# Where a decoder layer turns the 128 tiles of its expert table: eight moved into the first expert pass, fewer in earlier stages, and one input loaded ahead of a barrier

## The chip, the cores and the metric

The kernel runs on one core of one Trainium2 chip. The metric is the device time of one execution in microseconds (us). TensorE multiplies, VectorE, ScalarE and GpSimd (POOL) work on tiles in on-chip memory, and DMA transfers are issued from the queues of SyncE (SP), ScalarE and POOL.

## The reference

One layer of a decoder for 512 prompt tokens and 32 sample tokens (544 columns), then a final norm.

```python
h = rmsnorm(x, norm_mix)
proj = h @ w_in                        # feeds three branches and their gates
h_ml = mlstm_chunkwise(...)            # (A) matrix memory, 4 heads
y_rw, ... = rwkv7_branch(...)          # (B) 8 heads, ends with a norm by groups
y_xa = memory_attention(q, mk, mv)     # (C) mk, mv = projections of rmsnorm(mem_prompt)
x = x + jnp.sum(gates * bproj, axis=2) @ w_out
x = x + peer(rmsnorm(x, norm_ffn), pk_wq, pk_k1, pk_k2, pk_u, pk_v)

def peer(...):                         # per token, 8 heads
    v1, i1 = top_k(s1, 16); v2, i2 = top_k(s2, 16)
    top, pos = top_k(cand, 16)         # 16 of the 16384 experts per head
    gate = softmax(top)
    act = gelu(einsum('thkd,td->thk', u_tab[eidx], xb))
    return einsum('thk,thkd->td', gate * act, v_tab[eidx])
```

## The kernel before, in words

Five instruction streams, one an engine, are written out by hand and meet at semaphores. The stages follow each other, four of them closed by a barrier of all engines:

1. First branch (mLSTM): projections, a convolution on VectorE in eight steps, then a loop over four heads. `exponents(0)` on VectorE opens that loop.
2. Second branch (RWKV-7): chunks on small matrices, the sample tokens, then a norm by groups for each of four pairs of heads (`ym`, `xq`, `yv`, `g` on TensorE).
3. Memory attention: it loads the memory tokens (`MEM`, 1 MB), squares them on ScalarE, norms and projects them.
4. Gates, merge and output projection.
5. Queries: for 16 half heads TensorE makes queries and scores, and VectorE selects the best 16 (`choose(i)`, of which `top16` is the work). `choose(0)` to `choose(13)` stand here; in steps 1 to 8 VectorE also makes one low part of the layer's input (`XL`).
6. First pass: 128 slots. The kernel computes 416 tokens densely: tile `s` of the expert table `u` (512 KB) is loaded by SP into a ring of three buffers (`RAW`), split into a high half by ScalarE (`HI`) and a low half by VectorE (`low_part`, `LO`), two slots ahead of its 24 products on TensorE. `low_part` frees the ring's buffer for the next load. Beside that VectorE finishes the top-k for five groups of tokens (`top_part`, eight parts each, placed by `part_slot`), and 104 units of one-hot matrices (`one_hots`, placed by `hots_slot`) go from VectorE to ScalarE to TensorE and back through ScalarE into a gate table of 13 x 2 MB.
7. Second pass: the same with table `v`, 128 slots.

For the last 128 tokens the first pass doesn't use the dense product: their experts' rows are gathered and multiplied on VectorE (`dot`, 128 of them, spread by `dotted_by`). Gathering wants rows, and the input holds `u` by columns. So every one of the 128 tiles of `u` is also turned: POOL loads it (`turn_tiles`), VectorE transposes it by blocks (`turn_tile`), and POOL writes it to the table `u_rows` in four DMAs. That is side work laid into all the stages before the first gather. `TILES` says how: per phase the first tile, how many, and how many buffers they go through (depth). `turn_tile` waits for its tile's load and for the writes of the tile `depth` before it; the load in turn waits until that tile is turned. VectorE works in order, so a `turn_tile` that waits holds all that is written behind it.

Line 1657 is the transposition, 520 and 525 are POOL's load and writes of it, 1060 every product, 2125 `low_part`, 2092 to 2102 `top16`, 2258 `one_hots`, 2267 `dot`.

## Time and profile before

| | us |
|---|---|
| median of 3 runs | 2743.36 |
| lowest, highest | 2740.65, 2758.79 |
| the profiled execution | 2741.5 |
| its span, first to last instruction | 2739.8 |
| TensorE, VectorE, ScalarE, POOL busy | 2399.8, 1724.2, 913.8, 695.7 |

All rows come from the one profiled execution. Its time is 1.7 us above its span, and a saving read from the rows is taken off its time. Busy times are shares over stages with different limits: that VectorE is busy for 63% of the span says nothing about a stage in which it is the last to finish. In the rows "idle before" is how long the engine stood before the instruction, with what ended that.

### The profile page before, as it was taken

To read this page: it belongs to the slowest core of one execution; us is meant where nothing else is said; L and a number is where in the kernel's file an instruction comes from. 1 tells how busy PE (TensorE), PEld (TensorE's weight loads), DVE (VectorE), ACT (ScalarE), POOL (GpSimd) and SP (SyncE) were. 2 spreads that over 40 slices of the span, in tenths; PEclk is the share of its full clock that TensorE was granted. 3 is DMA by queue.
4 is the path that set the end of the run, shared out by engine and by line. 5 is a ranking of instruction groups with operands and counts; after the bars stand their busy time and mean duration, and the time that the engine had idled before them with its cause. 6 is when DMAs were issued, how large, how long until landed. Compare 5 with 4: busy or idle time off the path is not lost.

```text
span 2739.8 us, 41344 instructions
## 1 busy us (share of the span) xinstructions
PE 2399.8 (88%) x16321; PEld 2205.8 (81%) x16321; DVE 1724.2 (63%) x3186; ACT 913.8 (33%) x1569; POOL 695.7 (25%) x1011
## 2 busy tenths in 40 slices
PE   7956886887567989889669978999999999999997
PEld 5944665885456988878569977999999999999997
DVE  3545266434542444445878877777876577787876
ACT  3212143220011111122124455767775333333332
POOL 3310000001330555424520100333333123232320
PEclk9967897996787999999889989999999999999999
DMA  4620320012653899748655544999999889999993
GB/s 145 188 82 16 105 54 24 19 34 82 237 180 103 278 289 301 249 143 260 219 189 190 180 143 141 307 332 332 321 323 365 294 304 338 346 350 347 341 346 125
DMA packets 324337, 590.67 MB, mean 216 GB/s; under 512 B 26832, under 2 KB 217312, under 8 KB 322608
## 3 DMA queue, kind: packets, MB, share of 16 engines
q1 hardware_dynamic: 222960, 274.07, 30.5%
q0 software_dynamic: 82752, 286.69, 30.4%
q10 hardware_dynamic: 18432, 27.27, 2.7%
q8 instruction: 130, 2.13, 0.3%
q14 instruction: 63, 0.52, 0.1%
HBM read 459.28 MB, written 128.64 MB: 215 GB/s over the span
## 4 chain that ended last, share of the span: by engine, by line
PE 50%; DVE 22%; DMA 15%; issue 5%; ACT 5%; POOL 3%; ACTq 0%; DVEq 0%; POOLq 0%
PE PS L1060 49%; DMA GU<-u_rows,EIDX 4%; DMA RAW<-in_uT 3%; DMA u_rows<-arena 3%; DMA u_rows<-CBLK 3%; DVE arena L1623 3%; POOL u_rows L525 3%; DVE OH L2258 2%; DVE LO L2125 2%; DVE GU L2267 1%; DMA u_rows<-TQ 1%; ACT HI L964 1%; ACT OH L1002 1%; DVE arena L1657 1%; ACT arena L691 1%
## 5 line engine op out<-in xcount | busy, mean ns | idle before, releaser
L2125 DVE TENSOR_TENSOR LO<-RAW,HI 128x1024 fp32r<-128x1024 f32 x256 | 313.1, 1224 | 239.6 <-ACT HI L964 239.0
L964 ACT ACTIVATE HI<-RAW 128x1024 fp32r<-128x1024 f32 x256 | 270.1, 1056 | 538.8 <-PE PS L1060 508.7
L1060 PE MATMUL PS<-XH,HI 128*128 128x416 f32 x1024 | 373.5, 365 | 39.8 <-issue 39.8
L1060 PE MATMUL PS<-HT,W 128*128 128x272 f32 (+1 forms) x1536 | 381.0, 410 | 18.5 <-DVE HT L1669 12.4
L1060 PEld LDWEIGHTS PS<-HT,W 128*128 128x128 f32 (+1 forms) x1536 | 296.4, 194 | 96.9 <-issue 18.4
L1060 PE MATMUL PS<-XH,LO 128*128 128x416 f32 x1024 | 366.2, 358 | 0.0
L1060 PE MATMUL PS<-XL,HI 128*128 128x416 f32 x1024 | 364.2, 356 | 0.0
L1060 PE MATMUL PS<-WH,HI 128*128 128x416 f32 x1024 | 361.0, 353 | 2.0 <-DVE WL L2140 2.0
L1060 PE MATMUL PS<-WL,HI 128*128 128x416 f32 x1024 | 360.3, 352 | 0.0
L1060 PE MATMUL PS<-WH,LO 128*128 128x416 f32 x1024 | 358.0, 350 | 0.0
L1060 PE MATMUL PS<-arena 64*64 64x64 f32 (+10 forms) x3864 | 276.5, 260 | 69.3 <-DVE arena L1623 23.8
L1060 PEld LDWEIGHTS PS<-arena 64*64 64x64 f32 (+3 forms) x3864 | 220.2, 153 | 112.7 <-DVE arena L1623 30.2
L660 POOL DMA_INDIRECT GU<-u_rows,EIDX x128 | 157.9, 1233 | 567.0 <-DVE ACTG L2267 488.2
L668 POOL DMA_INDIRECT GROW<-in_vT,EIDX x128 | 155.3, 1213 | 408.1 <-DVE ACC L2283 311.5
L1060 PEld LDWEIGHTS PS<-XH,HI 128*128 128x128 f32 x1024 | 197.5, 193 | 42.1 <-issue 40.2
L1060 PEld LDWEIGHTS PS<-XL,HI 128*128 128x128 f32 x1024 | 197.5, 193 | 2.8
L1060 PEld LDWEIGHTS PS<-XH,LO 128*128 128x128 f32 x1024 | 196.2, 192 | 2.1
L1060 PEld LDWEIGHTS PS<-WH,HI 128*128 128x128 f32 x1024 | 192.5, 188 | 4.2 <-issue 2.3
L1060 PEld LDWEIGHTS PS<-WH,LO 128*128 128x128 f32 x1024 | 193.1, 189 | 2.4
L1060 PEld LDWEIGHTS PS<-WL,HI 128*128 128x128 f32 x1024 | 192.7, 188 | 1.1
L2267 DVE CUSTOM_DVE_ANT_0 GU<-GU,XTOK 128x1024 f32<-128x1024 f32 x128 | 155.2, 1222 | 57.4 <-DMA GU<-u_rows,EIDX 57.0
L1002 ACT ACTIVATE OH<-OH,IT 128x128 f32<-128x128 f32 x416 | 131.7, 391 | 154.1 <-DVE OH L2258 153.2
(261 smaller groups left out, 3647.3 us busy)
## 6 DMA issues: line engine op xcount, KB each, us to landing
RAW<-in_uT SPq DMA_DIRECT2D x128, 512.0 KB, 5.0
RAW<-in_vT SPq DMA_DIRECT2D x128, 512.0 KB, 5.8
arena<-in_uT POOLq DMA_DIRECT2D x92, 512.0 KB, 5.1
W<-in_w_in SPq DMA_DIRECT2D x58, 512.0 KB, 4.9
u_rows<-arena POOLq DMA_DIRECT2D x228, 128.0 KB, 3.9
table_a<-AX ACTq DMA_DIRECT2D x128, 208.0 KB, 4.6
gate_table<-GST SPq DMA_DIRECT2D x13, 2048.0 KB, 14.3
AIN<-table_a SPq DMA_DIRECT2D x128, 208.0 KB, 6.6
```

The lines of the kernel that those rows point to most:

```text
L525: pool.dma_start(rows[q], turned[32 * q:32 * q + 32].rearrange("c (b x) -> c b x", b=4)).then_inc(S(f"tout{k % 2}"), 16)
L660: pool.indirect_dma_start(out=GU[j % NGU][0:NGT], out_offset=None, in_=flat_u, in_offset=bass.IndirectOffsetOnAxis(ap=EIDX[0:NGT, 1, j:j + ...
L668: pool.indirect_dma_start(out=GROW[0:NGT, j % NGR, :], out_offset=None, in_=flat_v, in_offset=bass.IndirectOffsetOnAxis(ap=EIDX[0:NGT, 0, ...
L691: step(nc.scalar.activation(out, in_, func, **kw), sem)
L964: nc.scalar.activation(HI[:, s % NRING], RAW[:, s % NRING], ACT.Copy).then_inc(S("hi"), 1)
L1002: ins = nc.scalar.activation(hot, hot, ACT.Copy, scale=IT[:, 2, 4 * u + x:4 * u + x + 1])
L1060: return nc.tensor.matmul(out, lhsT, rhs, start=first, stop=last)
L1623: step(dve.tensor_tensor(out, x, y, op), sem)
L1657: dve.transpose(y.rearrange("p (b k r) -> p b k r", b=4, k=DT), x.rearrange("p (k b r) -> p b k r", k=DT, b=4)).then_inc(S("tr"), 1)
L2125: dve.tensor_tensor(LO_[:, s % NRING], RAW[:, s % NRING], HI[:, s % NRING].bitcast(F32), ALU.subtract).then_inc(S("lo"), 1)
L2258: ins = dve.tensor_tensor(OH[:, u % NOH, i], bc(iota[:], 1, 4), bc(IT[:, i, 4 * u:4 * u + 4], 2, P), ALU.is_equal)
L2267: dve.tensor_tensor_reduce(out=row, in0=row, in1=XTOK[0:NGT], scale=1.0, scalar=0.0, op0=ALU.mult, op1=ALU.add, accum_out=ACTG[0:NGT, j:j ...
```

## The change

It moves tiles between phases. The first stage turns 10 in place of 13, the second 4 + 10 as before, memory attention 12 in place of 11, gates and merge 58 as before, the query stage 26 in place of 32. The remaining eight are tiles 6 to 13 of the table: a new phase `E` turns them out of the first pass's own ring, where they stand anyway, in slots 4 to 11, and nothing loads them a second time. `tile_chunk` keeps the numbers straight.

In the query stage one tile is turned inside each of the first 12 selections (`top16(sets, between)`) and one after each of the 14; before, three stood after each of the first four and two after each of the others.

The ten tiles of the second branch's end become two phases, `S` (2) and `N` (8), turned at the same places. Between them POOL loads the memory tokens, now to a place of their own at `low - 4 * D`, as soon as the last product of the sample states (`ss3`) is made; before, that load stood behind barrier 2.

In the first pass the top-k parts come four slots later (`part_slot`: slots 10 to 57), the one-hot units start at slot 44 in place of 34 and end at 118 in place of 117, and 24 of the 128 dots are placed before the last part's end in place of 12.

```diff
 NGU = 3
-TILES = {"M": (0, 13, 1), "R": (13, 4, 1), "N": (17, 10, 2), "A": (27, 11, 2), "G": (38, 58, 2), "Q": (96, 32, 2)}
+TILES = {"M": (0, 10, 1), "R": (10, 4, 1), "S": (14, 2, 2), "N": (16, 8, 2), "A": (24, 12, 2), "G": (36, 58, 2),
+         "Q": (94, 26, 2), "E": (120, 8, 2)}
+E_FROM = 6
 assert sum(n for _, n, _ in TILES.values()) == NK
...
+def tile_chunk(i):
+    first, n, _ = TILES["E"]
+    if i >= first:
+        return E_FROM + i - first
+    return i if i < E_FROM else i + n
 def part_slot(t, part):
-    return 6 + 10 * t + part
+    return 10 + 10 * t + part
...
-    return part_slot(1, 7) + 11 + u * 84 // (8 * NEB)
+    return part_slot(1, 7) + 17 + u * 75 // (8 * NEB)
...
-    first, even, early = part_slot(0, 7) + 5, part_slot(NPT - 1, 7) + 3, 12
+    first, even, early = part_slot(0, 7) + 5, part_slot(NPT - 1, 7) + 3, 24
     if s < even:
...
                     "Q": [TQ[:, 2], TQ[:, 3]]}
-        tile_in["N"] = tile_in["G"] = tile_in["A"]
-        tile_out["N"] = tile_out["G"] = tile_out["A"]
+        for phase in ("S", "N", "G"):
+            tile_in[phase], tile_out[phase] = tile_in["A"], tile_out["A"]
+        tile_out["E"] = tile_out["Q"]
...
-        (MEM, MN, MKT, MV, PA, PAT, KB, VBM, XM, PM, PT3, c1, c2, c3, _) = carve(
-            0, (DT, NMEM), (DT, NMEM), (MH, NMEM), (2, 512), (2, 4, NMEM), (2, 512), (2, NB * NMEM),
+        (MN, MKT, MV, PA, PAT, KB, VBM, XM, PM, PT3, c1, c2, c3, _) = carve(
+            0, (DT, NMEM), (MH, NMEM), (2, 512), (2, 4, NMEM), (2, 512), (2, NB * NMEM),
             (2, NB * NMEM), (MH, NB, TS), (2, MH, NB, TS), (2, P), (4,), (4,), (4,))
+        MEM, _ = carve(low - 4 * D, (DT, NMEM))
         XQ = BR[:, 8:12]
...
                         pool.wait_ge(S("tr"), k + 1)
-                    if i < first + n:
-                        pool.dma_start(tile_in[phase][(i - first) % depth], a["uT"][:, i].rearrange("p k n -> p (k n)")
-                                       ).then_inc(S(f"tin{i % 2}"), 16)
+                    if i < first + n and phase != "E":
+                        pool.dma_start(tile_in[phase][(i - first) % depth],
+                                       a["uT"][:, tile_chunk(i)].rearrange("p k n -> p (k n)")).then_inc(S(f"tin{i % 2}"), 16)
                     if k >= first:
-                        rows, turned = u_rows[k].rearrange("(b c) q x -> q c b x", b=4), tile_out[phase][(k - first) % depth]
+                        rows, turned = u_rows[tile_chunk(k)].rearrange("(b c) q x -> q c b x", b=4), tile_out[phase][(k - first) % depth]
                         for q in range(4):
...
             pool.wait_ge(mm, NO[f"y{NC - 1}"] + 1)
+            turn_tiles("S")
+            pool.wait_ge(mm, NO[f"ss{RP - 1}"] + 1)
+            pool.dma_start(MEM, a["memT"].rearrange("(k p) t -> p k t", p=P)).then_inc(S("in0"), 16)
             turn_tiles("N")
...
-            pool.dma_start(MEM, a["memT"].rearrange("(k p) t -> p k t", p=P)).then_inc(S("in0"), 16)
             for r in range(2):
...
             turn_tiles("Q")
+            turn_tiles("E")
...
                 turned_tiles[0] += 1
-                dve.wait_ge(S(f"tin{i % 2}"), 16 * (i // 2 + 1))
-                k = i - depth
-                if k >= first:
+                k, y = i - depth, tile_out[phase][(i - first) % depth]
+                if phase == "E":
+                    s = tile_chunk(i)
+                    x = RAW[:, s % NRING]
+                    dve.wait_ge(S(f"raw{s % NRING}"), 16 * (s // NRING + 1))
+                else:
+                    x = tile_in[phase][(i - first) % depth]
+                    dve.wait_ge(S(f"tin{i % 2}"), 16 * (i // 2 + 1))
+                if k >= first or phase == "E":
                     dve.wait_ge(S(f"tout{k % 2}"), 64 * (k // 2 + 1))
-                x, y = tile_in[phase][(i - first) % depth], tile_out[phase][(i - first) % depth]
                 dve.transpose(y.rearrange("p (b k r) -> p b k r", b=4, k=DT), x.rearrange("p (k b r) -> p b k r", k=DT, b=4)
...
                 turn_tile("M")
-            for _ in range(5):
+            for _ in range(2):
                 turn_tile("M")
...
             dve.sem_inc(S("svbk"), 1)
-            turn_tile("N")
+            turn_tile("S")
             ps = take(dve, "us")
...
             dve.sem_inc(S("su"), 1)
-            turn_tile("N")
+            turn_tile("S")
             ps = take(dve, "ys")
...
                 tt(XM[:, h], bc(XQ[:, h, TP:T], 1, NB), bmask[:], sem=S("masked") if h == MH - 1 else None)
-            for _ in range(7):
+            for _ in range(8):
                 turn_tile("A")
...
-            def top16(sets):
+            def top16(sets, between):
...
                 step(ins)
+                if between:
+                    turn_tile("Q")
                 for x, y, vals, idx in sets:
...
                 step(top16([(SC[0:m, i % 4, t, :], SC2[0:m, i % 4, t, :],
-                             V16[0:m, t, i, :], IX[0:m, t, i, :]) for t, (_, m) in enumerate(PTILES)]), S("scf"))
+                             V16[0:m, t, i, :], IX[0:m, t, i, :]) for t, (_, m) in enumerate(PTILES)], i < 12), S("scf"))
...
                         ins.then_inc(S("xsplit"), 1)
-                for _ in range(3 if i in (0, 1, 2, 3) else 2):
-                    turn_tile("Q")
+                turn_tile("Q")
...
                     weigh_act(e + 2)
+                if 0 <= s + 2 - E_FROM < TILES["E"][1]:
+                    turn_tile("E")
                 if s + 2 < 2 * NK:
```

In the orders below `arena`, `CBLK` and `TQ` are the places of tiles and `in_uT` the table `u` by columns. Line numbers of after are some 12 to 21 higher for the same statement.

POOL's queue from the end of the second branch to the memory stage, before:

```order
88 L621 DMA out_shift<-arena 128x126
89 L623 DMA out_S<-arena 128x256
90 L520 DMA arena<-in_uT 128x1024 x3
91 L525 DMA u_rows<-arena 32x4x256 x4
92 L520 DMA arena<-in_uT 128x1024
93 L525 DMA u_rows<-CBLK 32x4x256 x4
...
107 L525 DMA u_rows<-CBLK 32x4x256 x4
108 L627 DMA out_Ss<-arena 128x2048
109 L631 DMA arena<-in_memT 128x8x256
110 L638 DMA arena<-in_memkT 128x2048 x2
111 L642 DMA arena<-in_memv 128x2048 x2
```

The third tile is loaded as soon as the first is turned, and the memory tokens are loaded last, behind the output `out_Ss`. The same place after:

```order
83 L635 DMA out_S<-arena 128x256
84 L532 DMA arena<-in_uT 128x1024 x2
85 L537 DMA u_rows<-arena 32x4x256 x4
86 L537 DMA u_rows<-CBLK 32x4x256 x4
87 L639 DMA arena<-in_memT 128x8x256
88 L532 DMA arena<-in_uT 128x1024 x3
89 L537 DMA u_rows<-arena 32x4x256 x4
90 L532 DMA arena<-in_uT 128x1024
91 L537 DMA u_rows<-CBLK 32x4x256 x4
```

Behind the two `S` tiles POOL now writes both out, loads the memory tokens, and only then the next tiles.

VectorE in the query stage, from inside one selection into the next, before:

```order
770 L2098 MAX arena<-arena 128x8 x4
771 L2098 MAX arena<-arena 32x8
772 L2101 MAX_INDEX arena<-arena 128x8
...
781 L2102 MAX_INDEX arena<-arena 32x8
782 L1657 STREAM_TRANSPOSE TQ<-TQ 128x1024 x3
783 L2092 MAX arena<-arena 128x8 x4
784 L2092 MAX arena<-arena 32x8
```

Three tiles stand in a row between two selections. After:

```order
771 L2118 MAX arena<-arena 128x8 x4
772 L2118 MAX arena<-arena 32x8
773 L1677 STREAM_TRANSPOSE TQ<-TQ 128x1024
774 L2123 MAX_INDEX arena<-arena 128x8
...
783 L2124 MAX_INDEX arena<-arena 32x8
784 L1677 STREAM_TRANSPOSE TQ<-TQ 128x1024
785 L2112 MAX arena<-arena 128x8 x4
786 L2112 MAX arena<-arena 32x8
```

One tile now lies between the second `MAX` and the places of the maxima, and one behind the selection.

VectorE in the first pass, from slot 3 to the first part, before:

```order
1046 L2125 TENSOR_TENSOR LO<-RAW,HI 128x1024 x5
1047 L2146 CAST arena<-arena 128x256
1048 L2150 TENSOR_TENSOR arena<-arena 128x8x16
...
1053 L2155 MAX arena<-arena 128x8 x8
1054 L2125 TENSOR_TENSOR LO<-RAW,HI 128x1024
1055 L2162 MATCH_REPLACE arena<-arena 128x54 x8
```

Splits stand alone until the parts begin. After:

```order
1059 L2146 TENSOR_TENSOR LO<-RAW,HI 128x1024 x2
1060 L1677 STREAM_TRANSPOSE TQ<-RAW 128x1024
1061 L2146 TENSOR_TENSOR LO<-RAW,HI 128x1024
1062 L1677 STREAM_TRANSPOSE TQ<-RAW 128x1024
1063 L2146 TENSOR_TENSOR LO<-RAW,HI 128x1024
1064 L1677 STREAM_TRANSPOSE TQ<-RAW 128x1024
```

In front of each of eight splits stands a tile turned out of the ring.

## Rows read from the trace of the kernel before

**Rows 1.** The chain in order of time: start us, us, what
```profile
1233.88 4.62 DMA u_rows<-TQ
...
1293.46 6.80 DMA u_rows<-TQ
...
1351.43 39.77 issue
...
2131.11 581.50 PE PS L1060 x3072
```

**Rows 2.** Timeline, end of the first stage: start us, us, engine, line, what, [idle before]
```profile
131.31 1.25 DVE L1657 STREAM_TRANSPOSE arena<-arena 128x1024 f32<-128x1024 f32 x1 [5.91 <-DMA u_rows<-arena]
...
136.50 0.98 PE L1064 MATMUL PS<-ident,BR 4*128 4x4 f32 x15
...
139.48 0.22 ACT L695 ACTIVATE arena<-PS 128x64 f32<-128x64 f32 x1
...
155.24 1.25 DVE L1657 STREAM_TRANSPOSE arena<-arena 128x1024 f32<-128x1024 f32 x1 [5.91 <-DMA u_rows<-arena]
...
156.81 2.00 DVE L1629 TENSOR_SCALAR arena<-arena 128x512 f32<-128x512 f32 x5
```

**Rows 3.** Timeline around the load of the memory tokens
```profile
667.58 1.25 DVE L1657 STREAM_TRANSPOSE arena<-arena 128x1024 f32<-128x1024 f32 x1
...
675.40 0.73 DVE L1984 TENSOR_SCALAR rstd<-PS 128x544 f32<-128x544 f32 x1 [6.57 <-PE PS L1060]
...
724.67 0.91 POOL L631 DMA_DIRECT2D arena<-in_memT  x1 [4.20 <-POOLq L410]
...
730.99 1.91 ACT L691 ACTIVATE arena<-arena 128x2048 f32<-128x2048 f32 x1 [16.73 <-DMA arena<-in_memT]
```

**Rows 4.** Timeline of VectorE, query stage; its waits for DMA from 1223 to 1392
```profile
1239.77 1.01 DVE L2092 MAX8 arena<-arena 128x8 f32<-128x128 f32 x5
...
1246.05 0.59 DVE L2115 TENSOR_TENSOR XL<-HT,XH 128x416 fp32r<-128x416 f32 x1
1246.56 2.36 DVE L1657 STREAM_TRANSPOSE TQ<-TQ 128x1024 f32<-128x1024 f32 x2
1254.81 1.25 DVE L1657 STREAM_TRANSPOSE TQ<-TQ 128x1024 f32<-128x1024 f32 x1 [5.88 <-DMA u_rows<-TQ]
...
DVE TQ L1657 <- DMA u_rows<-TQ: 36.3, 11, 7.0
```

**Rows 5.** First pass in stretches, TensorE (xcount) first: instructions on LO, then on OH
```profile
1552.00:1727.00 175.00, 65.61 (x178) 35.85 (x177) 28.19 (x23) 0.90 0.49 152
1727.00:2131.00 404.00, 201.27 (x568) 107.18 (x567) 85.68 (x70) 0.99 0.95 334
...
1552.00:1727.00 175.00, 35.30 (x224) 31.41 (x224) 36.94 (x58) 36.66 (x116) 0.90 0.49 152
1727.00:2131.00 404.00, 79.70 (x608) 78.08 (x608) 95.40 (x150) 95.04 (x300) 0.99 0.95 334
```

**Rows 6.** Timeline of VectorE in a slot with a unit and a part
```profile
1604.47 1.23 DVE L2125 TENSOR_TENSOR LO<-RAW,HI 128x1024 fp32r<-128x1024 f32 x1 [1.15 <-ACT HI L964]
1605.62 4.49 DVE L2213 TENSOR_TENSOR arena<-arena,iota 128x2048 f32<-128x2048 f32 x2
1610.14 1.29 DVE L2258 TENSOR_TENSOR OH<-iota,IT 128x512 f32<-128x512 f32 x2
1613.72 1.23 DVE L2125 TENSOR_TENSOR LO<-RAW,HI 128x1024 fp32r<-128x1024 f32 x1 [2.29 <-ACT HI L964]
```

**Rows 7.** A stretch of 4 us; last columns: TensorE clock, DMA share, GB/s
```profile
664.00:668.00 4.00, 4.00 (x9) 2.97 (x10) 3.22 (x5) 0.00 (x0) 0.00 (x0) 0.50 0.02 4
```

**Rows 8.** Timeline of VectorE at the start of the memory stage
```profile
746.36 1.25 DVE L1657 STREAM_TRANSPOSE arena<-arena 128x1024 f32<-128x1024 f32 x1
...
769.74 1.25 DVE L1657 STREAM_TRANSPOSE CBLK<-arena 128x1024 f32<-128x1024 f32 x1 [2.52 <-DMA u_rows<-CBLK]
...
778.46 1.22 DVE L1635 TENSOR_REDUCE arena<-PS 128x4 f32<-128x1024 f32 x1 [3.77 <-PE PS L1060]
```


## Prediction

> **What bounds the kernel now.** I read four views in this order: the chain that ended last, the timeline of each stage that the change touches, the waits, and the stretches. The chain in order of time already says that no one engine bounds the program: it runs through the writes of turned tiles in the query stage, through a stretch of TensorE with nothing to do at its end, and through TensorE alone in the second pass [rows 1]. So each stage has its own limit, and the change has to be priced stage by stage, by the wait that ends last there.
>
> At the end of the first stage VectorE turns five tiles that no longer lie beside other work: the tenth is turned at 131.31, the thirteenth at 155.24, and only then do the exponents of head 0 start, at 156.81, although ScalarE's copy of their input had ended at 139.48 + 0.22 = 139.7 [rows 2]. At the start of the memory stage everything waits for the load of the memory tokens: issued at 724.67, used at 730.99 [rows 3]. In the query stage VectorE is the bound: TensorE has finished at 1351.43 and stands for 39.8 us until VectorE has split the first tile [rows 1], and 36.3 us of VectorE's own time there are waits for the writes of turned tiles [rows 4]. In the second pass TensorE is the bound: 581.50 us for 128 tiles, 4.54 us each [rows 1]. In the first pass it is too, but for the stretch from 1552 to 1727, where top-k parts and one-hot units meet on VectorE [rows 5, 6].
>
> **The change part by part.**
>
> *First stage, three tiles fewer.* The tenth tile is done at 131.31 + 1.25 = 132.6. TensorE has the gate rows turned at 136.50 + 0.98 = 137.5, so VectorE now waits for TensorE and then for ScalarE's copy, and starts the exponents at 139.7 in place of 156.81: 17.1 us. ScalarE's exponentials now follow its copies without a pause, and what it did in the old gap comes in between; I take 0.5 us for that, an estimate. Term: **-16.6** (ends -19 and -12). What is late next is the copy itself, and then the loop over heads, whose pace does not change. This part is out of any cover: the whole gap is on the path.
>
> *Memory input loaded early.* The load moves from behind the barrier to behind the last state product (TensorE ends it near 664), on the same POOL queue, ahead of the eight N tiles. ScalarE's square can start when the barrier opens: 730.99 - 724.67 = 6.3 us. Behind the moved load on POOL's queue stand the first two N tiles, which used to be loaded tens of us earlier; VectorE comes to the first at 667.58 and, having turned it, waited for TensorE until 675.40 anyway, 6.57 us of idle [rows 3]. The load took 5.4 us from the end of its issue to its use, so issued at 664 to 665 it lands near 670, and the tile 1 to 3 us behind it, since DMA is nearly idle there (0.02 of its time in 664 to 668) [rows 7]. It has until 675.40 - 1.25 = 674.1: covered; if the tile were 3 us later than that, 3 us would be lost. Term: **-6.3** (ends -6.3 and -3).
>
> *Memory stage, eight tiles in front in place of seven.* They go in pairs through two buffers. The first stands at 746.36, the sixth at 769.74, and VectorE is ready for the scores at 778.46 after 3.77 us of idle [rows 8]. The sixth comes 23.4 us after the first, in two and a half turnarounds, 9.4 each; the eighth therefore comes at 769.74 + 9.4 = 779.1 and ends 1.25 us later, at 780.4, against 778.46. I take **+2.4** for it, with the uneven pairs in mind (ends 0 and +5). It eats part of the 6.3 won just before.
>
> *Query stage, 26 tiles in place of 32, spread.* One selection is 1246.05 - 1239.77 = 6.28 us, the split part 0.51, a turned tile 2.36 / 2 = 1.18 [rows 4]. Fourteen selections, eight split parts and 32 tiles are 87.9 + 4.1 + 37.8 = 129.8, with the 36.3 of waits 166.1 us; back from the first split, at about 1390, that puts the first selection at 1224, where it stands. Now six tiles go (7.1 us), and the question is what becomes of the waits. Today tiles come two or three in a row and the third waits 5.88 us for its buffer [rows 4]: its predecessor's four writes take up to 4.62 to 6.80 us to land after their issue [rows 1], so a buffer comes round in 8.3 us (1246.56 to 1254.81) to about 10.6 us. In the new order one tile lies inside a selection and one behind it, so a buffer is wanted again after 6.28 + 0.51 + 2.36 = 9.15 us for the steps with a split part, 8.64 for four others. That clears the shortest round and not the longest. I take 0.3 us of wait a step over twelve steps, 4 us, since evenly spread writes no longer queue behind each other. Saved: 7.1 + 36.3 - 4 = **-39.4** (ends -43 and -25, the latter at 1.5 us a step). The first product would start at 1391.2 - 39.4 = 1351.8. TensorE's own query work ended at 1351.43 even with its waits for the selections, so it is just covered; that is what is late next, and why no more than 43 can come.
>
> The Trainium skill, "DMA: Bandwidth & Descriptors", section on the anatomy of one DMA, gives a fixed cost of about 2 us and the rest by bytes over 436 GB/s; a write of 128 KB would by that estimate land after 2.3 us, and the round would be near 6 us. By that rule no wait at all is left and the sum is 4 us lower. The trace disagrees for now, with its 4.62 and 6.80; how much of it is queueing, no row of before shows.
>
> *Eight tiles turned out of the first pass's ring.* They cost VectorE 8 x 1.18 = 9.4 us in slots 4 to 11, where a slot is 4.54 us of TensorE's time and VectorE has one split (1.2 us) and no part before slot 10: nothing. In slots 10 and 11 they share the slot with a part; two slots of lead absorb it. Eight loads of 512 KB go, worth nothing where DMA is half idle. Their 32 writes come before the first gather.
>
> *Parts four slots later, units ten slots later and closer, 24 early dots in place of 12.* Between 1552 and 1727 TensorE made 178 / 8 = 22.3 tiles and 224 / 8 = 28 units [rows 5]. At 4.54 a tile and at most 1.07 a unit (what the 404 us after it leave for 608 / 8 = 76 units beside 568 / 8 = 71 tiles) that is 131 us: 44 us too long. The reason is the round in a slot with a unit: split 1.14, part (here 4.49), one-hots 1.29, then 2.29 us idle until ScalarE has scaled them and made the next high half, 9.25 in all [rows 6], so 4.73 plus the part. Eight parts are worth (175 - 22.3 x 4.73 - 6 double units x 1.2) / 2 = 31 us. Before, 16 parts met units; now the last four of one tile group and eight of the next. New: slots 44 to 57 cost VectorE 14 x 4.73 + 5 x 1.2 + 16 + 31 = 119 us against 14 x 4.54 + 19 x 1.07 = 84 of TensorE: 35 too long. Slots 20 to 43, without units, cost 24 x 1.14 + 31 + 31 + 15 + 13 dots x 1.22 = 120 against 109: 11 too long, of which a lead of some 8 hides most. So 38 to 46 in place of 44, and after it ten gathers of 0.5 MB fewer where DMA is the busiest. Term: **-2** (ends -15 and +12).
>
> **Sum.** -16.6 - 6.3 + 2.4 - 39.4 - 2 = -61.9. From the profiled execution's 2741.5 us: 2679.6. That execution lies 1.9 us below the median of the three runs (2743.4), inside their spread. Forecast: **2680 us**, 2.3% faster.
>
> **Rivals.**
>
> *The query loop stays bound by its buffers.* If a round stays at 10.6 us however the tiles are spaced, each of twelve steps waits 1.5 us, 18 us in place of my 4: 2694. For it: the late rounds of the query loop are the long ones. Against: these are rounds in which two tiles were written back to back.
>
> *The first pass gives time back.* Double the early dots, so VectorE's lead is gone by slot 35 and TensorE idles in short gaps; and units at 1.39 a slot in place of 1.24 leave less slack for the two gate-table stores that hold a tile's load up. At +12 instead of -2: 2694. Both together: 2708.
>
> *The first pass gains.* Fewer slots with part and unit at once, fewer gathers at the end: at -15, 2667.
>
> *Slower than before.* A ring tile stands in front of the next split on VectorE and waits for the write of the tile two before it. Two slots are 9.1 us; beyond that everything in the pass waits. If those writes took L us to land, four rounds would lose about L - 5 each. It needs L of 20 us to undo the 62, and 27 us to be slower by over 1%. Against it: 4.62 to 6.80 in the query stage, and a pass whose DMA queues are half idle at that point. It would give 2770.
>
> **How the numbers follow.** Forecast case 0.55; buffers 0.15; first pass gives back 0.14; first pass gains 0.11; ring tiles block 0.02; the remaining 0.03 are other losses under 1%. The range takes the two single rivals on either side and the bounds of the smaller terms: 2661 to 2704. A measurement of this kernel can tell about 1% (27 us) from no change; the forecast is 62 us, so faster by over 1% 0.94, within 1% 0.04, slower 0.02.
>
> **What would show it.** Right: the exponents of head 0 near 140; the square of the memory tokens directly behind the barrier, near 724.7 - 16.6; an idle of under 4 us between the eighth front tile and the scores; waits of VectorE for TQ writes under 10 us in place of 36.3, and TensorE's gap before the first pass 5 us in place of 39.8; the first pass 735 to 750 us long. Wrong: a wait for TQ writes in slots 4 to 11, a first N tile turned later than its idle allowed, or a first pass over 750 us.

## The result and the profile after

| | us |
|---|---|
| changed kernel, median of 4 runs | 2661.66 (2658.94 to 2666.59) |
| kernel before, 4 runs beside it | 2742.01 (2739.38 to 2758.79) |
| ratio | 0.9696, 95% interval 0.9655 to 0.9738 |
| span of the profiled execution | 2660.3, granted clock 0.939 |
| forecast | 2680, range 2661 to 2704 |

The change is faster by 3.0%, some 80 us where 62 were forecast; the time lies at the very low end of the range, and by the ratio, times the 2743.4 us of the kernel before on record, it is 2660.0, just below it. Spans fell by 79.5 us (2739.8 to 2660.3). Where they fell is read from marks that both traces have, so that every line is a difference of two starts (us from the span's start):

| mark | before | after | won so far | won here | on record |
|---|---|---|---|---|---|
| first stage's output (`out_cn`) issued | 295.5 | 275.1 | 20.4 | 20.4 | 16.6 |
| `out_S` issued, second branch | 620.8 | 597.9 | 22.9 | 2.5 | 0 |
| `out_Ss` issued, ahead of barrier 2 | 719.9 | 699.1 | 20.8 | -2.1 | 0 |
| `GWH` first written, gates | 879.8 | 852.1 | 27.7 | 6.9 | 3.9 |
| query stage begins (`KSEL` loaded) | 1196.8 | 1171.0 | 25.8 | -1.9 | 0 |
| first product on `XL`, first pass | 1391.7 | 1330.5 | 61.2 | 35.4 | 39.4 |
| second pass begins | 2131.1 | 2053.0 | 78.1 | 16.9 | 2 |
| end | 2739.8 | 2660.3 | 79.5 | 1.4 | 0 |

Every other stage came out within some 4 us of its term. The first pass did not: it fell from 739.4 to 722.4 us, and it alone holds 15 of the missing 18. The misses of the other stages mostly cancel. No run shows why the second branch won 2.5 us, and two of the marks depend on the profile. From `out_S` to `out_Ss` after took 101.2 us and before 99.1, while the eleven kernels below with after's code there (`mem_late` but for one load) took 94.6 to 101.4: the -2.1 is inside that spread. And the query stage, 159.5 us here, took 155.8 to 157.0 in the nine kernels below with the same code there: 38 to 39 us less than before, in place of 35.4.

**End of the first stage.** The timeline of after, the rows that answer to [rows 2]:

```profile
131.05 1.25 DVE L1677 STREAM_TRANSPOSE arena<-arena 128x1024 f32<-128x1024 f32 x1 [5.92 <-DMA u_rows<-arena]
...
139.11 0.22 ACT L710 ACTIVATE arena<-PS 128x64 f32<-128x64 f32 x1
...
139.48 1.92 DVE L1644 TENSOR_SCALAR arena<-arena 128x512 f32<-128x512 f32 x5 [1.93 <-ACTq L774]
...
144.50 7.57 PE L1075 MATMUL PS<-HT,W 128*128 128x272 f32 x32 [1.33 <-DVE arena L1766]
```

The tenth tile is the last, VectorE waits for ScalarE's copy, and the exponents start at 139.48 in place of 156.81: 17.3 us. The last line is the output gate of head 0. Before, the same 32 products stood here, ahead of them TensorE's stop:

```profile
156.83 2.50 PE L1060 MATMUL PS<-arena 128*128 128x384 f32 x4 [15.33 <-DVE arena L1721]
...
161.91 9.79 PE L1060 MATMUL PS<-HT,W 128*128 128x272 f32 x32 [1.03 <-DVE arena L1746]
```

They took 2.2 us longer. The stretches say why; columns as in [rows 7], first before, then after:

```profile
144.00:148.00 4.00, 0.00 (x0) 0.00 (x0) 0.00 (x0) 0.00 (x0) 0.00 (x0) 0.50 1.04 365
148.00:152.00 4.00, 0.00 (x0) 0.00 (x0) 1.25 (x1) 0.00 (x0) 2.38 (x5) 0.50 0.32 55
164.00:168.00 4.00, 4.00 (x14) 3.15 (x13) 0.88 (x4) 0.00 (x0) 0.00 (x0) 0.70 0.01 2
```

```profile
140.00:144.00 4.00, 3.17 (x10) 1.71 (x8) 3.79 (x8) 2.83 (x6) 0.00 (x0) 0.73 1.19 303
144.00:148.00 4.00, 3.50 (x15) 2.96 (x16) 3.33 (x12) 0.00 (x0) 0.00 (x0) 1.00 0.32 76
```

Through the idle stretch of before and until past 164 the granted clock was 0.50 (1.2 GHz); after, where TensorE stood only briefly, it is back at 1.00 (2.4 GHz) by 144. So the exponents came 17.3 us later in before, and the work behind the stop took some 2 to 3 more.

**Memory stage.** POOL, VectorE and ScalarE in the timeline of after, to be held against [rows 3]:

```profile
644.18 0.91 POOL L639 DMA_DIRECT2D arena<-in_memT  x1 [23.84 <-PE PS L1075]
```

```profile
651.73 1.25 DVE L1677 STREAM_TRANSPOSE arena<-arena 128x1024 f32<-128x1024 f32 x1 [4.46 <-DMA arena<-in_uT]
654.85 0.73 DVE L2004 TENSOR_SCALAR rstd<-PS 128x544 f32<-128x544 f32 x1 [1.87 <-PE PS L1075]
```

```profile
703.34 1.91 ACT L706 ACTIVATE arena<-arena 128x2048 f32<-128x2048 f32 x1 [10.13 <-POOLq L422]
```

The load of the memory tokens is issued 59 us ahead of its use and the square waits only for the barrier. The first N tile now has VectorE wait for its load, 4.46 us, and TensorE is still later by 1.87: that wait is covered, as forecast. In front of the scores the timeline of VectorE, against [rows 8], has

```profile
750.25 1.25 DVE L1677 STREAM_TRANSPOSE CBLK<-arena 128x1024 f32<-128x1024 f32 x1 [2.96 <-DMA u_rows<-CBLK]
751.42 1.19 DVE L1650 TENSOR_REDUCE arena<-PS 128x4 f32<-128x1024 f32 x1
```

The scores started 47.5 us behind the start of the square before (778.46 - 730.99) and start 48.1 behind it now (751.42 - 703.34), without any idle time between tile and scores. The eighth tile cost 0.6 us, not 2.4, as far as one profile of each can tell.

**Query stage.** The wait that answers to the last of [rows 4], VectorE from 1190 to 1331, and the chain in order of time, from 1195 to 1340, against [rows 1]:

```profile
DVE TQ L1677 <- DMA u_rows<-TQ: 7.6, 6, 3.0
```

```profile
1194.78 126.86 PE PS L1075 x615
1321.64 8.40 issue
1330.04 10.09 PE PS L1075 x44
```

Waits for the writes fell from 36.3 to 7.6 us and TensorE's stop ahead of the first pass from 39.8 to 8.4. In the first pass the ring tiles waited twice for a buffer, 2.4 us together. The forecast had named such a wait as a sign of being wrong; it cost nothing, since TensorE's products of slots 0 to 33 took 156.1 us against 156.4 before.

**First pass.** Slots 34 to 57, then 58 to the end (after; TensorE's instructions on `LO`, then on `OH`), read as [rows 5]:

```profile
1486.00:1647.00 161.00, 69.46 (x193) 37.27 (x192) 29.30 (x24) 0.94 0.58 183
1647.00:2053.00 406.00, 198.28 (x560) 105.57 (x560) 84.56 (x69) 1.00 0.93 325
...
1486.00:1647.00 161.00, 23.06 (x152) 21.16 (x152) 24.05 (x38) 23.86 (x76) 0.94 0.58 183
1647.00:2053.00 406.00, 86.91 (x682) 85.36 (x680) 107.60 (x170) 107.20 (x340) 1.00 0.93 325
```

By the prices on record (4.54 us a tile, 1.07 a unit) the first stretch holds 193 / 8 = 24.1 tiles and 152 / 8 = 19 units, 109.5 + 20.3 = 130 us of TensorE's work in 161: 31 too long. The second holds 70 tiles and 85 units, 317.8 + 91.2 = 409 us in 406, and TensorE is busy for 397.9 of them: it is at TensorE's pace. So nearly all that is too long still lies in slots 34 to 57. What ended TensorE's waits there, first in before from 1552 to 1727, then in after from 1486 to 1647:

```profile
PE PS L1060 <- ACT OH L1002: 15.9, 8, 4.2
PE PS L1060 <- ACT GST L1011: 15.4, 7, 4.2
```

```profile
PE PS L1075 <- ACT GST L1026: 22.0, 7, 7.4
PE PS L1075 <- DVE LO L2146: 1.7, 1, 1.7
PE PS L1075 <- ACT OH L1017: 1.3, 1, 1.3
```

So TensorE hardly ever stood for a tile (`LO`). It stood for ScalarE's work on the units: their scaling (`OH`) and the copy of an earlier unit out of TensorE's result memory (`GST`). These waits are 31 of the 44 us too long in before and 25 of the 31 after. The other 13 and 6 us lie in its products, at a mean granted clock of 0.90 and 0.94.

### The profile page after: what moved, and what is told of

Same layout as the page of the kernel before. It is cut to its first block, busy times and chain, and to the rows that moved or that the text cites. A ratio compares the mean times of both kernels' runs of the same rounds, so it can differ in the third digit from the quotient of the medians.

```text
span 2660.3 us, 41336 instructions
## 1 busy us (share of the span) xinstructions
PE 2383.6 (90%) x16321; PEld 2195.8 (83%) x16321; DVE 1722.8 (65%) x3186; ACT 914.0 (34%) x1569; POOL 693.2 (26%) x1003
## 4 chain that ended last, share of the span: by engine, by line
PE 44%; DVE 13%; DMA 10%; ACT 3%; POOL 2%; issue 2%; ACTq 0%; DVEq 0%; POOLq 0%
PE PS L1075 43%; DMA u_rows<-arena 3%; DVE LO L2146 2%; DMA RAW<-in_uT 2%; DMA u_rows<-CBLK 2%; DMA GU<-u_rows,EIDX 2%; DVE OH L2279 2%; POOL u_rows L537 2%; DVE GU L2288 2%; ACT OH L1017 1%; ACT HI L979 1%; DVE arena L2243 1%; DVE arena L1677 1%; DVE arena L2234 1%; DVE arena L1638 1%
## 5 line engine op out<-in xcount | busy, mean ns | idle before, releaser
L1075 PE MATMUL PS<-HT,W 128*128 128x272 f32 (+1 forms) x1536 | 374.9, 405 | 18.5 <-DVE HT L1689 12.5
```

What stands on the lines that cost most here:

```text
L1075: return nc.tensor.matmul(out, lhsT, rhs, start=first, stop=last)
```

## The experiments

Twelve kernels, each timed beside the kernel before. A number like 0.9938 is the ratio to before with its 95% interval; the changed kernel's is 0.9696, and two kernels are compared by their ratios, times 2742. The changed kernel's interval is 11 us wide to either side, so a difference of up to some 12 us from it isn't shown by the times alone; it is read from stages in the traces, one profile each. Lengths of stretches of slots are from TensorE's first product of one slot to that of another.

### The first pass's schedule, taken apart

`sched_only`, the kernel before with three lines:

```diff
-    return 6 + 10 * t + part
+    return 10 + 10 * t + part
-    return part_slot(1, 7) + 11 + u * 84 // (8 * NEB)
+    return part_slot(1, 7) + 17 + u * 75 // (8 * NEB)
-    ... part_slot(NPT - 1, 7) + 3, 12
+    ... part_slot(NPT - 1, 7) + 3, 24
```

> The kernel before with the schedule of the first pass alone changed: top-k parts from slot 10, one-hot units from slot 44 at 75 per 104, 24 early dots. The record (ledger of the first pass: 38 to 46 us too long in place of 44) expects 2740 us. Theory U, that the later units are worth more than the ledger gave them because parts and units share fewer slots, expects the first pass at 722 to 726 us in place of 739 and the time at 2726 to 2730. Theory R, that the eight fewer tile loads and the ring tiles are what shortened the pass, expects 2738 to 2744 here.

Measured 2726.94 us, 0.9938 (0.9918 to 0.9957): 17 us, between 12 and 22. The first pass took 728.0 us in the profile. Theory U's number; the record's ledger is refuted, and so is theory R, since this kernel turns no tile out of the ring.

`units_early`, the changed kernel with

```diff
-    return part_slot(1, 7) + 17 + u * 75 // (8 * NEB)
+    return part_slot(1, 7) + 7 + u * 84 // (8 * NEB)
```

> The changed kernel with its one-hot units back at their old slots (first at 34, 84 slots for 104 units, last at 117); parts and dots as changed. Theory U expects 9 to 17 us more than the changed kernel's 2661.7, so 2671 to 2679, nearly all of it between slots 34 and 62. The record's ledger expects at most 4 us more: 2662 to 2666. If the gain came from the dots or the ring, it stays at 2662.

Measured 2687.10, 0.9780 (0.9757 to 0.9803): 23 us more than the changed kernel's ratio, and even more than U expected; slots 34 to 61 took 28 us more (216.3 in place of 188.4). Its first pass is 748.6 us, longer than that of before: with units back at 34 and parts four slots later, 20 slots hold both, where before had 16.

`dots12`, the changed kernel with

```diff
-    first, even, early = part_slot(0, 7) + 5, part_slot(NPT - 1, 7) + 3, 24
+    first, even, early = part_slot(0, 7) + 5, part_slot(NPT - 1, 7) + 3, 12
```

> The changed kernel with 12 early dots in place of 24, so that 116 in place of 104 gathers of 0.5 MB stand behind slot 60. Theory G, that part of the first pass's gain behind slot 62 is fewer gathers beside the loads and the gate table's stores, expects 5 to 8 us more: 2667 to 2670. Theory U expects no change, 2660 to 2664. The record, which took the doubled early dots as a load on VectorE in slots 20 to 43, allows a gain of 1 to 3 us.

Measured 2671.83, 0.9744 (0.9720 to 0.9769): 13 us more, with intervals that overlap; its first pass, 736.2 us, is 8 to 14 longer than those of the kernels with the changed schedule. The start of slot 62 stands 345.1 us behind the first product (344.5 in the changed kernel), so the twelve extra early dots had cost nothing by then; the next 36 slots take 219 us in place of 210. VectorE's wait for gathered rows shows it, changed kernel first, then this one:

```profile
DVE GU L2288 <- DMA GU<-u_rows,EIDX: 32.5, 17, 4.6
```

```profile
DVE GU L2288 <- DMA GU<-u_rows,EIDX: 59.6, 39, 5.8
```

Behind slot 62 VectorE waits for gathers one at a time, and each dot brought forward is a wait less there. Theory G holds and is larger than it said. Against the kernel before, this one's pass is only 3.2 us shorter: slots 34 to 57 win 26 us (158.0 in place of 184.4), and the slots from 58 on, which take 11 units more, lose 23 of them (421.8 in place of 399.1). With the dots moved too they lose 7 (406.1).

`parts_early`, the changed kernel with parts at `6 + 10 * t + part`, units and dots at their absolute slots:

> The changed kernel with its top-k parts four slots earlier (slots 6 to 53) and units and dots at their slots as they are. Parts and units then share slots 44 to 53 in place of 44 to 57. Theory U, by which a slot with part and unit loses about 2 to 3 us, expects 5 to 10 us less: 2652 to 2657. The rival, that ring tiles and parts in the same slots 6 to 11 take VectorE's lead away, expects 3 to 6 us more: 2665 to 2668.

Measured 2652.45, 0.9659 (0.9640 to 0.9679): 10 us less than the changed kernel, with intervals that overlap, and a first pass 6 us shorter. Slots 34 to 61 take 178.2 us in place of 188.4, slots 0 to 33 take 158.0 in place of 156.1. Both theories are partly right: eight shared slots in place of twelve win 10 us, and parts this early beside ring tiles cost 2. The kernel before, with parts this early and no ring tiles, took 156.4.

So the three moves of the changed schedule are not of one sign. Undone one at a time in the changed kernel, parts four slots later were a loss of 10 us by the ratios (6 in the first pass), the units ten slots later a gain of 23, the twelve dots a gain of 13. They don't add up: together they would be 26 and gave 17, since what one is worth depends on the others.

### How far it goes

`units_54`, the changed kernel with

```diff
-    return part_slot(1, 7) + 17 + u * 75 // (8 * NEB)
+    return part_slot(1, 7) + 27 + u * 65 // (8 * NEB)
```

> The changed kernel with its units starting ten slots later still: first at slot 54, 65 slots for 104 units, last at 118. Four slots are left that hold part and unit, in place of fourteen. Theory U (a shared slot loses 2 to 3 us, 25 to 29 us in twelve to fourteen of them by the run with units from 34 and by parts from 6) expects 15 to 22 us less than the changed kernel: 2640 to 2647. The rival, that units at 1.6 a slot in place of 1.39 are limited by the gate table's stores or by the round from VectorE over ScalarE to TensorE, expects stretches of 6.8 us a slot and more behind slot 62, and 2660 to 2675.

Measured 2645.98, 0.9646 (0.9628 to 0.9665). Theory U. (The fourteen of the expectation were twelve: slots 48 and 49 hold no part.) The rival's limit was not met: slots 62 to 97 take 217.8 us, 6.05 each, where a tile and 1.6 units cost TensorE at most 4.54 + 1.6 x 1.07 = 6.25.

`apart`: parts at `6 + 10 * t + part`, dots where they were, and

```diff
-    return part_slot(1, 7) + 17 + u * 75 // (8 * NEB)
+    return part_slot(1, 7) + 31 + u * 65 // (8 * NEB)
```

> Parts from slot 6 (to 53) and units from slot 54: no slot holds both. Theory U expects the stretch from slot 34 to 62 at its lowest, some 155 to 162 us, and 2636 to 2645 in all. The rival is that the work on VectorE in slots 6 to 53 (splits, parts, ring tiles, early dots) is by itself over what TensorE needs there, so that it gains less than 5 us over the run with parts from 10 and units from 54.

Measured **2634.75** (2634.04 to 2636.07), 0.9598 (0.9583 to 0.9613), which beats both kernels: 110 us under before and, by the ratios, 27 under the changed kernel. Of these 21 lie in the first pass (701.3 us in place of 722.4); its first product came 6 us sooner by stages that it shares with the changed kernel. Slots 34 to 61 took 147.8 us, less than theory U's 155 to 162, and the rival falls: the pass is 8 us shorter than that of `units_54`. Its stretches of the same slots (TensorE on `LO`, then on `OH`):

```profile
1482.00:1606.00 124.00, 68.10 (x194) 36.31 (x193) 30.49 (x25) 0.99 0.65 218
1606.00:2025.00 419.00, 197.93 (x560) 105.35 (x559) 84.48 (x69) 1.00 0.93 321
```

```profile
1482.00:1606.00 124.00, 6.54 (x40) 6.07 (x40) 8.77 (x14) 7.97 (x26) 0.99 0.65 218
1606.00:2025.00 419.00, 99.99 (x792) 98.00 (x792) 121.86 (x194) 122.24 (x391) 1.00 0.93 321
```

24.3 tiles and 5 units are 115 us in 124: 9 too long, in place of 31 after and 44 before, though no slot holds both; TensorE's waits there are 6.5 us, 4.1 of them for the first unit. The 14 units more that moved behind slot 58 cost 419 - 406 = 13 us there, which is TensorE's price for them and no more. The wait of ScalarE for a unit's comparison, in before, the changed kernel and this one:

```profile
ACT OH L1002 <- DVE OH L2258: 153.2, 76, 8.1
```

```profile
ACT OH L1017 <- DVE OH L2279: 106.1, 57, 6.4
```

```profile
ACT OH L1017 <- DVE OH L2279: 64.0, 36, 10.6
```

The order of the program gives the mechanism. ScalarE works in order; a unit's scaling stands in front of the next tile's high half and of the copy of an earlier unit (`copy_unit`), and in a shared slot the comparison that the scaling waits for stands behind a part on VectorE. So the part delays the scaling, that delays high half and copy, and VectorE has to wait for the high half before its next split: each round is as long as both engines' work one behind the other. TensorE, in order too, then stands at its next unit. One such round in the changed kernel, VectorE, ScalarE and then TensorE:

```profile
1591.86 1.23 DVE L2146 TENSOR_TENSOR LO<-RAW,HI 128x1024 fp32r<-128x1024 f32 x1 [1.15 <-ACT HI L979]
1593.00 0.55 DVE L1653 COPY IT<-PS 128x384 f32<-128x384 f32 x1
...
1595.17 1.02 DVE L2186 MAX8 arena<-arena 32x8 f32<-32x54 f32 x8
1596.22 2.50 DVE L2279 TENSOR_TENSOR OH<-iota,IT 128x512 f32<-128x512 f32 x4
1601.02 1.23 DVE L2146 TENSOR_TENSOR LO<-RAW,HI 128x1024 fp32r<-128x1024 f32 x1 [2.29 <-ACT HI L979]
```

```profile
1597.56 1.61 ACT L1017 ACTIVATE OH<-OH,IT 128x128 f32<-128x128 f32 x5 [3.37 <-DVE OH L2279]
...
1599.07 0.97 ACT L1017 ACTIVATE OH<-OH,IT 128x128 f32<-128x128 f32 x3
1599.95 1.04 ACT L979 ACTIVATE HI<-RAW 128x1024 fp32r<-128x1024 f32 x1
1600.89 0.49 ACT L993 ACTIVATE AX<-PS 128x416 f32<-128x416 f32 x1
1601.29 1.03 ACT L1026 ACTIVATE GST<-PS 128x512 f32<-128x512 f32 x1
```

```profile
1602.47 1.13 PE L1075 MATMUL PS<-OH 128*128 128x128 f32 x8 [1.01 <-ACT GST L1026]
```

From split to split 9.2 us: the part until 1596.2, then the comparisons of two units, ScalarE's scaling of them, for whose start it stood 3.37 us, its high half at 1599.95, and only then VectorE's split, after 2.29 us of idle. TensorE's next unit waits for the copy that ends at 1602.3. Another order on ScalarE, with copy and high half ahead of the scaling, was not tried. In `apart`, in a slot with a part and no unit, the high halves of two tiles follow each other by 4.5 us, TensorE's pace, and each waits for TensorE alone:

```profile
1519.63 1.06 ACT L979 ACTIVATE HI<-RAW 128x1024 fp32r<-128x1024 f32 x1 [1.47 <-PE PS L1075]
...
1524.14 1.06 ACT L979 ACTIVATE HI<-RAW 128x1024 fp32r<-128x1024 f32 x1 [1.62 <-PE PS L1075]
```

`apart_ring3`, as `apart` and with

```diff
-E_FROM = 6
+E_FROM = 3
```

> As the run before, with the eight ring tiles taken from chunks 3 to 10 of the table, so turned in slots 1 to 8, ahead of most parts. With parts from slot 6 the first 34 slots took 7 us longer than with parts from 10; if that is ring tiles and parts on VectorE in the same slots, three fewer shared slots give 2 to 5 us back; if it is the parts alone (the kernel before had the same 164 us there without ring tiles), nothing changes.

Measured 2639.00, 0.9611 (0.9590 to 0.9632). A miss: the first 34 slots took 161.7 us, more than `apart`'s 158.2, and the time is not better; the whole first pass is the same (700.4 and 701.3). Sharing slots with parts is not what ring tiles cost there. Turned earlier they came while VectorE had little lead, two selections among them, and twice waited for the writes ahead of them, 9.2 us together. The splits of tiles 4 to 16 then started 1.2 to 3.7 us ahead of TensorE's use of the tile, where those of `apart` had up to 7.7.

`parts8_ring3`, parts from 8, units from 49 (`+ 24 + u * 70 //`), `E_FROM = 3`:

> Parts from slot 8 (to 55), units from slot 49 at 70 slots for 104, ring tiles from chunk 3. Between the changed kernel and the runs with part and unit apart: seven shared slots in place of fourteen. Theory U expects 2648 to 2654; if the rate of units behind slot 62 is what limits (1.49 a slot here, 1.6 in the others), it is the fastest of the four at 2645.

Measured 2648.77, 0.9645 (0.9629 to 0.9661), where theory U put it.

The schedules in a line, by the number of slots that hold a part and a unit (first pass from its first product on `XL` to the second pass's first product, one profile each; "early" is the number of early dots; `parts8_ring3` and `apart_ring3` also turn their ring tiles earlier):

| shared slots | kernel | early | first pass, us |
|---|---|---|---|
| 20 | units_early | 24 | 748.6 |
| 16 | before | 12 | 739.4 |
| 12 | dots12 | 12 | 736.2 |
| 12 | changed; sched_only | 24 | 722.4; 728.0 |
| 8 | parts_early | 24 | 716.4 |
| 7 | parts8_ring3 | 24 | 715.8 |
| 4 | units_54 | 24 | 709.3 |
| 0 | apart; apart_ring3 | 24 | 701.3; 700.4 |

At 24 early dots a shared slot is worth (748.6 - 701.3) / 20 = 2.4 us on average; at 12 early dots the step from 16 to 12 slots is worth only 0.8 each. The profiles of three more kernels below, with the changed schedule, gave 724.1 to 727.8, so a single profile is good to some 3 us.

### The other parts

`query_grouped`, the changed kernel with

```diff
-                if between:
-                    turn_tile("Q")
...
-                turn_tile("Q")
+                for _ in range(2 if i < 12 else 1):
+                    turn_tile("Q")
```

> The changed kernel with its 26 query tiles grouped again: two after each of the first twelve selections, one after the last two, none inside a selection. If the spacing is what removed the waits for turned tiles' writes (36.3 us before, 7.6 after), 12 pairs wait again, 2 to 3 us a pair: 2685 to 2695 with TensorE's gap ahead of the first pass back at 30 to 40 us. The rival, that only the third tile in a row ever waited and pairs fit through two buffers, expects 2662 to 2666.

Measured 2671.84, 0.9714 (0.9693 to 0.9734): 5 us more by the ratios, 8 in the trace (first product at 1338.5 in place of 1330.5). Its query stage took 167.0 us, 7.5 more than in the changed kernel's profile and 10 to 11 more than in the nine others. The chain has

```profile
1322.18 15.87 issue
```

in place of 8.40, and waits for TQ writes are 14.3 us in place of 7.6. The number lies between the theories, much nearer to the rival: going from three and two tiles in a row to two and one took most of the waits away (36.3 to 14.3), the spacing the rest.

`mem_late`, the changed kernel with the load of `MEM` behind barrier 2 again:

```diff
-            pool.dma_start(MEM, a["memT"].rearrange("(k p) t -> p k t", p=P)).then_inc(S("in0"), 16)
             turn_tiles("N")
...
             barrier(pool, 2)
+            pool.dma_start(MEM, a["memT"].rearrange("(k p) t -> p k t", p=P)).then_inc(S("in0"), 16)
```

> The changed kernel with the load of the memory tokens behind barrier 2 again, at its new place in memory. The record (6.3 us at the barrier) expects 2666 to 2669, the square of the memory tokens 6.3 us behind the barrier. The rival, that the early load costs the N tiles behind it as much as it saves, since the first of them now comes after 4.46 us of idle, expects 2660 to 2664.

Measured 2668.25, 0.9711 (0.9692 to 0.9729): 4 us more, less than the times can tell apart, and in the trace the square starts 7.2 us later,

```profile
710.55 1.91 ACT L706 ACTIVATE arena<-arena 128x2048 f32<-128x2048 f32 x1 [16.95 <-DMA arena<-in_memT]
```

while `out_Ss`, ahead of the barrier, is issued at 699.4 as against 699.1. The record's 6.3 holds, and no cost of the load to the N tiles is seen, though stages of the same code differ by some us between profiles. This kernel keeps POOL's wait for `ss3` ahead of the N tiles; whether that wait costs anything was not tried alone.

`first_13`, the changed kernel with 13 tiles in the first stage and five ring tiles:

```diff
-TILES = {"M": (0, 10, 1), ... "E": (120, 8, 2)}
+TILES = {"M": (0, 13, 1), ... "E": (123, 5, 2)}
-            for _ in range(2):
+            for _ in range(5):
                 turn_tile("M")
```

> The changed kernel with 13 tiles in the first stage and five, not eight, out of the ring. By the record's term for three tiles (16.6 us) it takes 2678. By theory C, that the shorter stop also keeps TensorE at its higher clock through the output gate of the first head (the stop has it at half clock from 139 to 166 before, to 142 after), it takes 19 to 21 us more: 2681 to 2683. If ring tiles cost something in the first pass, three fewer give 1 to 3 us back.

Measured 2686.97, 0.9773 (0.9755 to 0.9791): 21 us more, and `out_cn` 22.1 us later. Theory C, by the trace; the interval of the times would allow the record's term too. The gate of head 0 is slow again, behind a stop of 18.19 us.

```profile
165.06 10.35 PE L1075 MATMUL PS<-HT,W 128*128 128x272 f32 x32 [1.03 <-DVE arena L1766]
```

`ring_16`, the changed kernel with ten tiles in memory attention, twenty in the query stage and sixteen from the ring (slots 4 to 19):

> The changed kernel with sixteen tiles out of the ring in place of eight: ten in place of twelve in memory attention, twenty in place of twenty-six in the query stage (one inside each of the first twelve selections, one after each of the first eight). If ring tiles are free, the query stage ends 6 to 8 us sooner (TensorE's gap of 8.4 us ahead of the first pass is nearly all that is left there) and the memory stage 2 us: 2652 to 2655. If ring tiles in slots 12 to 19, which also hold parts of the top-k, take VectorE's lead away, the first pass gives 8 to 12 us back: 2660 to 2666.

Measured 2665.14, 0.9705 (0.9685 to 0.9725): no gain. The first pass began 7.4 us sooner (1323.1) and took 730.4 us, 8.0 more. Eight ring tiles in slots 4 to 11 were free (the first 34 slots take 156.1 us with them and 155.9 without, in `sched_only`); with eight more in slots 12 to 19 they take 162.1, 4.3 us of it in those same slots (40.6 in place of 36.3). That gives back the head start, of which the query stage itself, 154.9 us, had won 4.6 against the changed kernel's profile and 1 to 2 against the nine others.

## Why the prediction was off

*First stage, -16.6: right in mechanism, 4 short.* The exponents came 17.3 us sooner, as worked out. That the stop also kept TensorE at its lower clock through the next products was not priced; [rows 2] show no clock. It measured 20.4, and 22.1 when undone, behind a longer stop.

*Memory load, -6.3: right.* 6.9 together with the eighth tile, 7.2 at the square when undone. The N tile's cover held. *Eight front tiles, +2.4: too dear*, 0.6, as turnarounds got shorter. The 2.1 us lost ahead of the barrier are inside what kernels with the same code differ by there.

*Query stage, -39.4: right*, 35.4 in the one profile and 38 to 39 in nine others. The 4 us of waits allowed were 7.6. By the estimate of 2.3 us for a 128 KB write, from the Trainium skill, "DMA: Bandwidth & Descriptors", section "Anatomy of one DMA", no wait was to be left. The traces agree for `out_S`, a write of 128 KB with little else under way, which landed after 2.1 us before and 2.3 after. They disagree for the turned tiles' writes, which landed after a median of 4.4 us before and 4.2 after; six waits remain. Of the reason given ("evenly spread writes no longer queue behind each other") the grouped kernel shows that it is the smaller part: shorter groups, and six tiles fewer, did most of it.

*Ring tiles, 0: right.*

*First pass, -2: this step failed.* It measured -16.9 in the trace, and -17 (-22 to -12) with the schedule alone. The ledger had counted the shared slots rightly, 16 before and 12 after, and its 44 us too long before is what the marks give (184.4 us for slots 34 to 57, with 24 tiles and 30 units worth 141). Two things in it were wrong.

One is a term that was put too dear. "Slots 44 to 57 ... 119 us" took 113.1, 29 too long in place of 35, and slots 20 to 43, for which it allowed 3 to 11, were 2.5 too long (111.5 against 109). The ledger's sum, 38 to 46 too long in place of 44, could win 6 us at best; measured, 31 were left, 13 fewer. The plain proportion, 12 shared slots of 16 at 44 us, is 33. Its picture of the stretch, VectorE's round as the bound, was right as far as it went; that TensorE's waits end on ScalarE's scaling and copies, and that its clock is lower between them, was not in it.

The other is a term that was put at nothing: "ten gathers of 0.5 MB fewer where DMA is the busiest". It was written down without a price. With the dots left where they were the pass is 736.2 us, 3.2 under before, near the forecast's -2; the dots are worth 8 to 14 us more. They are what makes the eleven units more behind slot 58 cheap: that part of the pass took 399.1 us before, 421.8 in `dots12` and 406.1 after, where 11 x 1.07 = 12 more were due.

*The rivals.* "The first pass gains" (2667, chance 0.11) is what happened, for the reasons that it names, and the gain was a little over its -15. "The first pass gives time back" and "buffers stay bound" fell, and no ring tile blocked. The range fell short because its low end took in this one rival and left next to no room for the first stage's extra 4 us on top. That the rest of the sum came out near its -59.9 (62.6 in the trace) is partly luck: 4 us too little for the first stage, 3 for the memory stage and 2.5 for the second branch stand against 4 too much for the query stage and two losses of 2.

## What to carry to other kernels

Count the slots in which two kinds of side work meet on an in-order engine and price the meeting, not the work: here each cost some 2.4 us, while units alone ran at TensorE's pace and parts alone nearly so (`apart`'s slots 34 to 57 are still 9 us too long). Then look at what TensorE itself waits for there; here it was ScalarE's unit work, not the missing tile that the ledger suggests. A proportion from the trace (so much lost in so many such slots) was better than a ledger that adds up every instruction against a single slot's budget. And a change that bundles three moves of a schedule should be tried move by move: one of the three was a loss of 6 to 10 us, hidden under two gains, and the gains depend on each other.

## What the runs showed of the hardware

A stop of TensorE of 15.3 us at the end of the first stage cost more than its length: the granted clock was 0.50 in it and until past 164, over 7 us of work behind it, and 32 products took 9.79 us (10.35 in `first_13`) in place of 7.57.

Writes of turned tiles that are issued one tile at a time also wait, less often: six waits of up to 3.0 us for 26 tiles, as against eleven of up to 7.0 for 32. Their 128 KB writes landed after a median of 4.2 us, the 128 KB of `out_S`, with little else under way, after 2.3.

In the crowded slots 34 to 57 TensorE's short waits, none over 7.4 us, went with a mean granted clock, of its two levels 0.50 and 1.00, of 0.90 before, 0.94 after and 0.99 in `apart`.
